# One core, two transformer blocks: first features by halves, three weight rests on another engine, gate logs, last norm and last down tile in smaller pieces

## The reference

```python
# first block, first lines
a = rmsnorm(h, norm_mix_g[layer]); proj = a @ w_in[layer]
# second block, forget gates of the recurrence (f: 256 x 1024 for both directions)
return jax.nn.log_sigmoid(f), jax.nn.sigmoid(-f)
# second block, feed-forward and final norm
x = x + g1 * (o @ w_out[l])
h2 = modulate(rmsnorm_2(x, norm_ffn[l]), sh2, sc2)
a, g = jnp.split(h2 @ w_up, 2, axis=-1)
x = x + g2 * ((a * gelu(conv(g) + conv_b)) @ w_down)
return rmsnorm_2(x, norm_final)
```

## Time and profile before

| | us |
|---|---|
| median of 3 runs (lowest, highest) | 1891.03 (1890.95, 1891.30) |
| profiled execution, its own time | 1890.74 |
| its span | 1888.9 |
| TensorE busy | 1813.4 |
| VectorE, ScalarE, GpSimd busy | 1290.7, 923.0, 561.1 |
| mean granted TensorE clock, of full | 0.988 |

### The profile page before, as it was taken

The page is one execution under the profiler, slowest core; times in us unless marked ns, Lnnn a source line. Parts: engine busy times, 40 slices in busy tenths (PEclk is TensorE's granted clock), DMA queues, the critical chain, the costliest instruction groups (busy, mean ns, idle before and its releaser), DMA issues.

```text
span 1888.9 us, 33337 instructions
## 1 busy us (share of the span) xinstructions
PE 1813.4 (96%) x11416; PEld 1579.2 (84%) x11416; DVE 1290.7 (68%) x2359; ACT 923.0 (49%) x1283; POOL 561.1 (30%) x251
## 2 busy tenths in 40 slices
PE   6999999999999989999999999999999989979997
PEld 5889977896878889999999988888885876659996
DVE  2557497775424599367777588888886768757776
ACT  4466444533556534567777543333334464134444
POOL 5877733500568598800000000000000000003333
PEclk9999999999999999999999999999999999989999
DMA  5544432576344366755555676666668760245553
GB/s 183 194 163 146 164 116 100 186 247 240 119 167 154 133 195 208 221 170 179 171 176 173 213 259 237 237 236 236 238 236 280 253 229 1 86 149 189 181 185 111
DMA packets 122840, 347.66 MB, mean 184 GB/s; under 512 B 13904, under 2 KB 46800, under 8 KB 122512
## 3 DMA queue, kind: packets, MB, share of 16 engines
q1 hardware_dynamic: 121248, 339.52, 53.9%
q0 software_dynamic: 1520, 7.21, 1.0%
HBM read 328.84 MB, written 17.83 MB: 184 GB/s over the span
## 4 chain that ended last, share of the span: by engine, by line
PE 81%; DVE 7%; POOL 4%; ACT 4%; issue 3%; DMA 1%; POOLq 0%; SPq 0%; ACTq 0%; DVEq 0%
PE banks L912 80%; POOL weight_rest L822 4%; ACT arena L1522 2%; ACT weight_high L1522 1%; PE banks L923 1%; DVE ssd_rest L2082 1%; DVE arena L2259 1%; DMA weight_ring<-in_stream 1%; DVE weight_rest L2091 0%; DVE arena L2626 0%; DVE arena L2739 0%; DMA arena<-in_stream 0%; DMA small<-in_pos 0%; DVE small L2635 0%; DVE attention_rest L2318 0%
## 5 line engine op out<-in xcount | busy, mean ns | idle before, releaser
L1522 ACT ACTIVATE weight_high<-weight_ring 128x1024 fp32r<-128x1024 f32 x448 | 473.1, 1057 | 467.5 <-PE banks L912 389.5
L822 POOL TENSOR_TENSOR weight_rest<-weight_ring,weight_high 128x1024 fp32r<-128x1024 f32 x184 | 476.4, 2599 | 200.4 <-ACT weight_high L1522 109.0
L2091 DVE TENSOR_TENSOR weight_rest<-weight_ring,weight_high 128x1024 fp32r<-128x1024 f32 x264 | 323.1, 1225 | 174.5 <-ACT weight_high L1522 168.3
L912 PE MATMUL banks<-a_high,weight_high 128*128 128x256 f32 x1216 | 303.7, 288 | 0.1
L912 PE MATMUL banks<-a_rest,weight_high 128*128 128x256 f32 x1216 | 297.8, 283 | 0.0
L912 PEld LDWEIGHTS banks<-a_rest,weight_high 128*128 128x128 f32 x1216 | 233.0, 192 | 0.3 <-issue 0.2
L912 PEld LDWEIGHTS banks<-a_high,weight_high 128*128 128x128 f32 x1216 | 232.6, 191 | 0.6 <-ACT weight_high L1522 0.3
L912 PE MATMUL banks<-weight_high,gated_high 128*128 128x512 f32 x512 | 201.4, 393 | 0.0
L912 PE MATMUL banks<-weight_high,gated_rest 128*128 128x512 f32 x512 | 200.2, 391 | 0.0
L1522 ACT ACTIVATE arena<-banks 128x512 f32<-128x512 f32 (+4 forms) x241 | 160.9, 689 | 64.7 <-PE banks L912 62.7
L912 PE MATMUL banks<-a_high,weight_rest 128*128 128x256 f32 x1216 | 171.9, 284 | 12.4 <-POOL weight_rest L822 12.4
(11 more groups left out here) (316 smaller groups left out, 3202.3 us busy)
## 6 DMA issues: line engine op xcount, KB each, us to landing
weight_ring<-in_stream SPq DMA_DIRECT2D x512, 512.0 KB, 3.4
arena<-in_stream SPq DMA_DIRECT2D x66, 512.0 KB, 3.2
unit_spill<-small SPq DMA_DIRECT2D x128, 128.0 KB, 3.6
scratch<-unit_spill SPq DMA_DIRECT2D x128, 128.0 KB, 3.2
residual<-in_x SPq DMA_DIRECT2D x2, 512.0 KB, 4.0
arena<-in_mem POOLq DMA_DIRECT2D x2, 512.0 KB, 5.2
arena<-in_ctx POOLq DMA_DIRECT2D x2, 512.0 KB, 3.9
arena<-in_keys POOLq DMA_DIRECT2D x1, 1024.0 KB, 5.3
```

What stands on the lines that cost most here:

```text
L822: nc.gpsimd.tensor_tensor(w_lo[:, e % 2, :], raw(e)[0], w_hi[:, e % 2, :], ALU.subtract).then_inc(S["rest_ready"], 1)
L912: return nc.tensor.matmul(out, lhsT, rhs, start=start, stop=stop, skip_group_check=True)
L1522: return nc.scalar.activation(out, in_, f, **kw)
L2091: tt(w_lo[:, e % 2, :], raw(e)[0], w_hi[:, e % 2, :], ALU.subtract).then_inc(S[ready], 1)
```

## The change

Four places, in the order of the kernel. At the start, `rows` and positions are fetched behind the first two weight tiles, x has a semaphore for each tile, TensorE multiplies zeros six times (`keep_busy`), transposes by halves of the features, and VectorE makes the features by halves and the first three weight rests in between; GpSimd begins with rest 3 and waits for the third. In "in2", the pieces of gate log and K2 are cut into token halves and put between high copies. Before the feed-forward, squares are taken by blocks of 512, the high copy of token tile 0 stands ahead of the weight copies, features are made in eight 128-wide scalings from PSUM, zeroing stands ahead of the second transposes, and banks are changed. At the end, the last down tile goes through by token halves, its rest is VectorE's, and squares are by blocks.

```diff
     B.job("w2", 1, 1, bank=4)
     for r in range(2, 4):
-        B.job("gb", r)
-    for h in range(2):
-        B.job("x3T", 1, h)
+        B.job("gb", r, bank=3 + r)
...
+    B.job("x3T", 1, 0, bank=7)
+    B.job("x3T", 1, 1, bank=4)
...
-            sp.dma_start(rows[:, :], A["rows"].partition_broadcast(P)).then_inc(in_const, 16)
-            sp.dma_start(small[:, 616:618].bitcast(I32), A["pos"]).then_inc(in_const, 16)
...
+                if g == 1:
+                    sp.dma_start(rows[:, :], A["rows"].partition_broadcast(P)).then_inc(in_small, 16)
+                    sp.dma_start(small[:, 616:618].bitcast(I32), A["pos"]).then_inc(in_small, 16)
...
-            for e in range(8):
+            pool.wait_ge(S["rest_ready"], 3)
+            for e in range(3, 8):
                 split_rest(e)
...
             hidden_rest(("ae",), FC - 1, 1)
-            split_down(65)
...
+            def keep_busy(times):
+                for _ in range(times):
+                    mm(ps[:, 7, :], WARM[:, 0:P], WARM)
+
+            pe.wait_ge(S["warm_zeros"], 1)
+            keep_busy(5)
+            pe.wait_ge(in_const, 32)
...
-            norm_transposes("xT", XN, 0)
-            pe.wait_ge(S["x1_hi_ready"], 4)
-            pe.wait_ge(S["x1_lo_ready"], 4)
+            for h in range(2):
+                for t in range(TT):
+                    pe.wait_ge(S["xn_ready"], t + 1)
+                    transposes(("xT", t, h), [XN[:, t, hsl(4 * h + k)] for k in range(4)])
+            keep_busy(1)
+
+            def x1_parts(j):
+                if j % 2 == 0:
+                    both_ready("x1", 2 + j)
...
             gates_spread(1)
+            pe.wait_ge(S["zeros_ready"], 1)
+            for t in range(TT):
+                for h in range(2):
+                    mm(claim(("f", t, h)), ident, ZEROS, start=True, stop=False)
             normed_turned(1)
-            pe.wait_ge(S["act_ready"], 8)
...
+            def down_by_tokens(e, c, par):
+                pe.wait_ge(S["hidden_ready"], c + 1)
+                pe.wait_ge(S["hi_ready"], e + 1)
+                wh, wl = w_hi[:, e % 2, :], w_lo[:, e % 2, :]
+                for t in range(TT):
+                    x_hi, x_lo = hidden_hi[:, par, tsl(t)], hidden_lo[:, par, tsl(t)]
+                    for h in range(2):
+                        o, s = bank(("f", t, h)), slice(h * 512, (h + 1) * 512)
+                        mm(o, x_hi, wh[:, s], start=False, stop=False)
+                        mm(o, x_lo, wh[:, s], start=False, stop=False)
+                    if t == 0:
+                        pe.wait_ge(S["ffn_lo_ready"], 45)
+                    for h in range(2):
+                        filled(mm(bank(("f", t, h)), x_hi, wl[:, h * 512:(h + 1) * 512], start=False), ("f", t, h))
...
+                if m in (16, 18):
+                    t = (m - 16) // 2
+                    act.wait_ge(S["g_abs"], 1)
+                    func(LF[:, t, :], LF[:, t, :], ACT.Exp, scale=-1.0).then_inc(S["g_e"], 1)
+                if m in (19, 20):
+                    act.wait_ge(S["g_e"], m - 18)
+                    func(LF[:, m - 19, :], LF[:, m - 19, :], ACT.Ln, bias=1.0).then_inc(S["g_l"], 1)
+                if m in (22, 23):
+                    act.wait_ge(S["g_nk"], m - 21)
+                    func(K2[:, m - 22, :], K2[:, m - 22, :], ACT.Exp, scale=-1.0).then_inc(S["g_k"], 1)
...
-            act.wait_ge(S["x3_ready"], 2)
-            row_root(8, 0, hres[:, 0, :], XN[:, 0, :])
+            row_root(8, 0, "x3_ready")
+            x3_high(0)
             for r in range(2):
                 split_high(F0 + r)
-            x3_high(0)
+            row_root(8, 1, "x3_ready")
+            x3_high(1)
             gates_spread(1)
...
+            for h in range(2):
+                k = slice(4 * h, 4 * h + 4)
+                for t in range(TT):
+                    b = arrived(dve, ("xT", t, h)).rearrange("p (k n) -> p k n", k=4)
+                    free(tt(actT[:, k, tsl(t)], b, bc(col("g_mix")[:, k], 2, P), ALU.mult), ("xT", t, h))
+                if h == 1:
+                    split_rest(1, "rest_ready")
+                for t in range(TT):
+                    dve.wait_ge(S["x1_hi_ready"], 2 * h + t + 1)
+                    tt(x1_lo[:, k, tsl(t)], actT[:, k, tsl(t)], x1_hi[:, k, tsl(t)],
+                       ALU.subtract).then_inc(S["x1_lo_ready"], 1)
+                if h == 0:
+                    split_rest(0, "rest_ready")
+            split_rest(2, "rest_ready")
...
+            dve.wait_ge(in_small, 32)
...
+            for t in range(TT):
+                in2_rests(19 + t, 20 + t)
+                dve.wait_ge(S["g_l"], t + 1)
+                signal(stt(K2[:, t, :], gate[:, t, :], 0.0, LF[:, t, :], ALU.max, ALU.add), "g_nk")
+            for t in range(TT):
+                in2_rests(21 + t, 22 + t)
+                dve.wait_ge(S["g_nk"], t + 1)
+                signal(stt(LF[:, t, :], gate[:, t, :], 0.0, LF[:, t, :], ALU.min, ALU.subtract), "g_logf")
...
+                    b = arrived(dve, ("x3T", t, h))
+                    for k in range(4):
+                        f = 4 * h + k
+                        ins = ts(actT[:, f, tsl(t)], b[:, hsl(k)], modsb[:, 16 + f:17 + f], modsb[:, 24 + f:25 + f],
+                                 ALU.mult, ALU.add)
+                    free(ins, ("x3T", t, h))
...
             hidden_channels(("ae",), FC - 1, 1)
+            split_rest(F0 + 65, "ffn_lo_ready")
...
                     add_gated(("f", t, b), 1, T512[:, 2 * t + b, :], b, t, "x4_ready")
-            for t in range(TT):
                 row_mean(9, t)
+            for t in range(TT):
                 row_scaled(9, t, FIN2)
```

More of the change, by code:

```diff
@@ L518, in build @@
         h_in = [sem(f"units_loaded{s}") for s in range(4)]
-        in_x = sem("x_loaded")
+        in_x = [sem(f"x_loaded{t}") for t in range(TT)]
+        in_small = sem("rows_loaded")
         in_mem = sem("mem_loaded")
@@ L736, in build @@
         ZEROS = area(29696, 512)
+        WARM = ZEROS
         by_head = lambda ap: ap.rearrange("p (h d) -> p h d", d=SP_)
@@ L1513, in _ @@
             down(64, FC - 2, 0)
-            down(65, FC - 1, 1, last=True)
+            down_by_tokens(F0 + 65, FC - 1, 1)
         @block.scalar
@@ L1944, in _ @@
             split_high(I0 + 1)
-            split_blocks(I0, 7, block_and_more)
+            for m in range(2, N_IN2):
+                split_high(I0 + m)
+                if m % 4 == 1:
+                    block_and_more(m // 4 - 1)
+                if m in (16, 18):
[8 more added lines that the diff above has]
+                    func(K2[:, m - 22, :], K2[:, m - 22, :], ACT.Exp, scale=-1.0).then_inc(S["g_k"], 1)
             block_and_more(6)
@@ L2070, in features, with split_rest @@
                             signal(tt(o, o, bc(shift[:, 4 * h:4 * h + 4], 2, P), ALU.add), "act_ready")
-            dve.wait_ge(in_const, 64)
-            scale_rows(0, D, lambda t: hres[:, t, :], lambda t: XN[:, t, :])
-            features("xT", actT, col("g_mix"))
+            def split_rest(e, ready, turn=None, n=8):
+                i_ = 0 if turn is None else turn
+                dve.wait_ge(S["hi_ready"], i_ * n + (e + 1))
+                if e > 1:
+                    dve.wait_ge(S["hi_begun"], i_ * n + e)
+                tt(w_lo[:, e % 2, :], raw(e)[0], w_hi[:, e % 2, :], ALU.subtract).then_inc(S[ready], 1)
+            signal(V.memset(WARM, 0.0), "warm_zeros")
+            scale_rows(0, D, lambda t: hres[:, t, :], lambda t: XN[:, t, :])
+            dve.wait_ge(in_const, 32)
+            for h in range(2):
+                k = slice(4 * h, 4 * h + 4)
[8 more added lines that the diff above has]
+                       ALU.subtract).then_inc(S["x1_lo_ready"], 1)
+                if h == 0:
+                    split_rest(0, "rest_ready")
+            split_rest(2, "rest_ready")
             def rest_quarters(hi, lo_, hi_ready, ready, src=None, per=2):
@@ L2700, in x3_features @@
                 for h in range(2):
-                    b = arrived(dve, ("x3T", t, h)).rearrange("p (k n) -> p k n", k=4)
-                    o = actT[:, 4 * h:4 * h + 4, tsl(t)]
-                    free(tt(o, b, bc(modsb[:, 16 + 4 * h:20 + 4 * h], 2, P), ALU.mult), ("x3T", t, h))
-                    freed(dve, ("x3T", t, h))
-                    signal(tt(o, o, bc(modsb[:, 24 + 4 * h:28 + 4 * h], 2, P), ALU.add), "act_ready")
-                dve.wait_ge(S["x3_hi_ready"], t + 1)
-                tt(x3_lo[:, :, tsl(t)], actT[:, :, tsl(t)], x3_hi[:, :, tsl(t)],
-                   ALU.subtract).then_inc(S["x3_lo_ready"], 1)
+                    b = arrived(dve, ("x3T", t, h))
[4 more added lines that the diff above has]
+                    free(ins, ("x3T", t, h))
+                for h in range(2):
+                    dve.wait_ge(S["x3_hi_ready"], 2 * t + h + 1)
+                    q = (slice(None), slice(4 * h, 4 * h + 4), tsl(t))
```

(1 more changed line is left out.)

95 lines of the change are left out of this document (41 added, 54 removed).

## The result

| | before | after |
|---|---|---|
| median (lowest to highest), us | 1890.99 (1888.48 to 1891.30), 4 runs | 1867.31 (1864.29 to 1868.67), 4 runs |
| profiled execution, its span | 1890.74, 1888.9 | 1866.71, 1864.9 |
| mean granted TensorE clock | 0.988 | 0.995 |

The ratio is 0.9887 (95%: 0.9874 to 0.9900), 23.7 us less; 21.4 less was predicted. In a later set of rounds the changed kernel took 1869.62 beside 1888.84 of the kernel before: 0.9906 (0.9890 to 0.9923). The page's first line shows why totals of engines say little here: TensorE is as busy as in the earlier trace rows, with 8.6 us of products with zeros in it, and what went is waits and stretches at the lower clock.

A forecast was written before the change was run, and what follows sets the result against it. TensorE is busy 96% of the span, so only waits and half-clock stretches can go: start -6.2, gate logs -7.2, norm -7.1, end -0.9, sum -21.4, from the median 1891.03 to 1869.6 us; range 1863 to 1877.

The forecast's parts named there:

- the give-back: Start: of the 8.8 us gained at tile 3, 2.6 is lost again as ScalarE's sine waits for the rope angles.
- the hold: Start: GpSimd's rests 3 to 5 block VectorE's short rope steps, about 4 of 18 done at 26.5, angles at 29.7.
- Tile 17's expected wait of 0.5: Gate logs: TensorE still waits 0.5 us at tile 17 with ScalarE's pieces halved.
- tile 23's of 0.1: Gate logs: TensorE still waits 0.1 us at tile 23 with ScalarE's pieces halved.
- 0.4 by the ring: Gate logs: late weight transfers and ring slots cost 0.4 us, 3 at worst.
- the step that the zeroing, not the norm, would set the transposes: Before the feed-forward: zeroing ends at 1673.4, after the norm's 1671.95, so transposes start at 1673.4.
- the fall: Before the feed-forward: TensorE idles 3.6 us, the clock falls, and channel tile 0's products step at 0.213, not 0.12.
- That transposes don't help the clock: Before the feed-forward: transposes don't count as busy for the clock, so the eight at 1673.4 don't help hold it.
- no give-backs (1864): Rival, chance 0.16: rope steps not held, clock kept before the feed-forward, hidden rest in time; 2.6 + 2.1 + 1.0 less.
- more given back (1876): Rival, chance 0.17: tile 6's stop drops the clock (2.5), gate-log ring 3 us short, tile 0 lands as now (1.2).
- the ordering without effect: Rival, chance 0.04: ScalarE's pieces still stop TensorE, norm bound elsewhere; gate logs and norm give nothing, 1884.
- a clock that stays low: Rival, chance 0.03: the fillers don't hold and the clock stays lower after the earlier start; 1892 or more.

The follow-up runs named there:

- later sine kernel: Changed kernel with ScalarE's rope sine behind the second token block's evacuation, not the first's: 1868.68 us, ratio 0.9893.
- the second and third kernel: Kernel before with only the gate pieces changed (1883.83 us, 0.9974), and with only the norm before the feed-forward part changed (1879.65 us, 0.9960).

## Why the prediction was right

All four places gave what was forecast to 0.1 us, or up to 1.0 us more.

**The start.** Predicted -6.2, measured -7.24. The first product was expected at 12.8 and came at 12.43, tile 3 gained 9.20 (expected 8.8). The size of the give-back was off: the hold exists, and beside the three GpSimd rests three steps were held, yet three more had passed before the first and one passes in each gap, so that eight and not four of the 18 were done at 26.5; the angles were there at 28.7 and not 29.7, TensorE waited 1.37 us and not 2.1 with 0.6 behind. The later sine kernel shows that this was the give-back, 1.96 with all that hangs on it, where 2.6 was expected. The transposes' 0.21 us was rightly read as the lower level, but the run without the zeros shows only 0.6 us for all six.

**The gate logs.** Predicted -7.2, measured -7.1, and -6.8 alone. Tile 17's expected wait of 0.5 and tile 23's of 0.1 came as one of 0.25 at tile 20. That the sum is right to 0.1 is in part luck: of the 1.1 us that the 11 tiles take above 30.3 (2.85 each on the mean, not 2.75), only that 0.25 shows as a wait, by a late transfer, where 0.6 by the pieces and 0.4 by the ring were expected.

**The norm.** Predicted -8.9 at the first up product and -7.1 with the clock; measured -8.75 and -7.6. The step that the zeroing, not the norm, would set the transposes is right, and so is the fall in six of seven profiles. Its price was 1.5 us (20.04 against 18.55 in the one execution without it), not 1.8. That transposes don't help the clock, which made the fall surer, isn't borne out by the starts: in four of the five traces in which TensorE had done nothing but 16 transposes, the record begins with the higher level during them or up to 0.5 us behind them (at 14.24, 14.22, 15.23 and, without the zeros, 12.68), in the fifth only at 24.39. What I didn't see is that the order I costed was the worse one: I took the zeroing's new place as the gain, and it is a loss of 2.3 to 2.8 against its old place behind the faster norm.

**The end.** Predicted -0.9, measured -1.3. VectorE's weight rest shut GpSimd out for 0.85 us (expected 1.0), the first addition came 0.59 earlier (expected 0.4), and from it to the last scaling it is 7.01 us in place of 7.75 (expected 7.3).

The sum by place is -7.24 - 7.1 - 7.6 - 1.3 = -23.2; the two profiled spans differ by 24.0. The rest lies almost all between the attention's first product and tile 16 (1400.27 us against 1401.01), where the kernel before has two falls on record and the changed kernel one; that this is the cause isn't shown. That the later median of 1869.62 meets the forecast of 1869.6 is luck, since the first was 1867.31. Of the rivals, no give-backs (1864) is excluded at its three places, each of which shows its wait; more given back (1876) needed a fall at tile 6, and the clock stood at 1.00 there (it also put 2.5 us on a fall, and those measured cost 1.5); the ordering without effect is excluded by the second and third kernel, a clock that stays low by all of them.

## What to carry to other kernels

When a step is moved off the path, ask where idle time opens next, and put work that waits for nothing there: the zeroing cost 2.3 to 2.8 us ahead of the transposes, the clock's part included, against its place behind them. Measure such edits between marks inside the timeline, because falls of the clock that come and go by execution can move the total by more than the edit. A short chain on one engine that releases another engine's queue, as the rope angles do the sine, is best consumed as late as its user allows. Before trusting a granted clock in the first microseconds of a trace, hold it against the length of a product that also stands later in it.

## What the runs showed that was not expected

- The clock's falls come and go at the same place. Behind the same 3.73 us wait for the rest of the features it fell in six of seven profiles and held in one; behind the 1.92 us wait at 104 to 106, which follows 3.00 us of transposes, it fell in six of the ten with the new start, as at 104 to 110 in the later sine kernel, with 0.87, 0.50 and 0.77 in its three stretches of 2 us. One costs about 1.5 us before the feed-forward (10.12 against 8.64 from the first up product to the next mark). With several such places they are the likely cause of most of the spread between executions of one kernel; what decides between fall and no fall, no run here shows.
- PEclk reads 1.00 ahead of the first change that a trace records, whatever the engine does: the first products of the kernel with the gates alone took 0.63 us there, and 0.39 once its record has the higher level.
- A VectorE step on 48 numbers takes 2.29 to 2.45 us beside a GpSimd operation of 2.40, but the next step passes in the 0.3 us between such operations. The other way round, a GpSimd operation of 0.72 us took 1.57 beside VectorE's 1.22.
